# An encoder of two layers: the first q block goes ahead of the gate ranks, and the first expert group's weights come in four stages

## The reference, cut to what matters

```python
h = concat([meta, x])
for i in range(2):
    hn = rms_norm(h, norm_mix[i])
    h = h + (conv_gla_mixer(hn, sc_w_in, ...) if i == 0 else gqa_axial_mixer(hn, att_w_in, ...))
    h = h + hierarchical_moe(rms_norm(h, norm_ffn[i]), ...)
return rms_norm(h, norm_final)

# conv_gla_mixer: one product, then split into parts
a_b, a_c, a_x, q, k, v, r, g_f, g_b = split(hn @ w_in)      # g_f, g_b: gate ranks, 16 columns each
log_a_f = log_sigmoid(g_f @ wg_f + bg_f) / 16               # and log_a_b likewise

# hierarchical_moe: top group of 4, top 2 of its 8 experts
for e in range(32):
    he = silu(xt @ w_gate[e]) * (xt @ w_up[e])              # 1024 -> 256
    out += gates[:, e:e+1] * (he @ w_down[e])               # 256 -> 1024
```

## Time and profile before

| | |
|---|---|
| median of 3 runs | 718.74 us (717.98 to 719.11) |
| the profiled execution | 717.45 us |
| its span, first to last instruction | 715.6 us |
| busy: PE, VectorE, ScalarE, GpSimd | 627.2, 267.9, 183.3, 58.0 us |
| PE's share of the span | 88% |
| moved by DMA | 233.35 MB, 326 GB/s over the span |
| chain that ended last | PE 68%, DMA 15%, SP's queue 10%, VectorE 4% |

### The profile page before, as it was taken

The page is one execution under the profiler, slowest core; times in us unless marked ns, Lnnn a source line. Parts: engine busy times, 40 slices in busy tenths (PEclk is TensorE's granted clock), DMA queues, the critical chain, the costliest instruction groups (busy, mean ns, idle before and its releaser), DMA issues.

```text
span 715.6 us, 11273 instructions
## 1 busy us (share of the span) xinstructions
PE 627.2 (88%) x4780; PEld 404.1 (56%) x4780; DVE 267.9 (37%) x608; ACT 183.3 (26%) x371; POOL 58.0 (8%) x39
## 2 busy tenths in 40 slices
PE   5999999989899999699489999998899996677774
PEld 3698999967566474274134345677556463244331
DVE  6346348742222333033033488913313230211213
ACT  4554444342101010010005347823211010000003
POOL 1222222300000000000001450000000000000000
PEclk9999999998999999899799999999899998899888
DMA  9972337985899999999997615069999999999994
GB/s 312 277 254 111 118 119 259 419 308 244 355 420 399 423 421 421 420 422 420 411 387 270 240 54 177 1 226 424 397 398 419 419 422 419 423 420 420 422 402 169
DMA packets 58815, 233.35 MB, mean 326 GB/s; under 512 B 14402, under 2 KB 14708, under 8 KB 37252
## 3 DMA queue, kind: packets, MB, share of 16 engines
q1 hardware_dynamic: 56532, 232.32, 81.7%
q10 hardware_dynamic: 2224, 0.20, 0.2%
HBM read 231.44 MB, written 1.05 MB: 325 GB/s over the span
## 4 chain that ended last, share of the span: by engine, by line
PE 68%; DMA 15%; SPq 10%; DVE 4%; issue 2%; ACT 1%; ACTq 0%; DVEq 0%
PE bank L1975 11%; DMA ring<-in_moe_w_up 7%; PE bank L2040 6%; PE bank L2064 6%; PE bank L2013 5%; PE bank L1639 5%; SPq L415 5%; PE bank L1641 5%; PE bank L1640 5%; PE bank L2027 4%; PE bank L2129 4%; DMA ring<-in_moe_w_gate 4%; SPq L412 3%; PE bank L1660 2%; PE bank L2137 2%; DMA w_g<-in_sc_w_in 2%
## 5 line engine op out<-in xcount | busy, mean ns | idle before, releaser
L1975 PE MATMUL bank<-ring,hnT 128*32 128x256 f32 (+1 forms) x1480 | 128.3, 425 | 37.8 <-DMA ring<-in_moe_w_up 13.1
L1975 PEld LDWEIGHTS bank<-ring,hnT 128*32 128x32 f32 x1480 | 64.7, 118 | 81.2 <-issue 37.4
L2064 PE MATMUL bank<-moe_scratch 128*128 128x512 f32 (+1 forms) x160 | 79.0, 617 | 3.7 <-DVE moe_scratch L1406 2.0
L1374 DVE TENSOR_TENSOR h<-bank,h 128x512 f32<-128x512 f32 (+1 forms) x80 | 55.1, 689 | 55.0 <-PE bank L2064 54.8
L2013 PE MATMUL bank<-ring,moe_scratch 128*32 128x512 f32 x404 | 58.6, 596 | 1.0 <-ACT moe_scratch L858 0.5
L2040 PE MATMUL bank<-sel,hn 128*128 128x256 f32 x240 | 59.0, 405 | 0.0
L2040 PEld LDWEIGHTS bank<-sel,hn 128*128 128x128 f32 x240 | 57.9, 336 | 0.0
L1639 PE MATMUL bank<-hnT_hi,mix_hi 128*128 128x272 f32 x192 | 57.1, 298 | 0.0
L1391 DVE TENSOR_TENSOR moe_scratch<-moe_scratch,bank 128x256 f32<-128x256 f32 x16 | 6.7, 421 | 134.0 <-ACT moe_scratch L856 134.0
L1641 PE MATMUL bank<-hnT_lo,mix_hi 128*128 128x272 f32 x192 | 55.6, 289 | 0.0
L1640 PE MATMUL bank<-hnT_hi,mix_lo 128*128 128x272 f32 x192 | 55.3, 288 | 0.0
(11 more groups left out here) (327 smaller groups left out, 930.7 us busy)
## 6 DMA issues: line engine op xcount, KB each, us to landing
ring<-in_moe_w_gate SPq DMA_DIRECT2D x45, 1024.0 KB, 25.8
ring<-in_moe_w_down SPq DMA_DIRECT2D x44, 1024.0 KB, 17.8
ring<-in_moe_w_up SPq DMA_DIRECT2D x41, 1024.0 KB, 23.9
ring<-in_sc_w_in SPq DMA_DIRECT2D x12, 1024.0 KB, 11.5
tail<-in_moe_w_up SPq DMA_DIRECT2D x7, 1024.0 KB, 25.1
ring<-in_moe_w_gate SPq DMA_DIRECT2D x13, 512.0 KB, 7.2
ring<-in_moe_w_up SPq DMA_DIRECT2D x13, 512.0 KB, 8.3
ring<-in_moe_w_down SPq DMA_DIRECT2D x13, 512.0 KB, 18.1
```

Source lines behind the costliest of these rows:

```text
L1374: nc.vector.tensor_tensor(hh, B[[7, 4][k % 2]][0:n, :], hh, ALU.add).then_inc(sem(f"h_added{l}"), 1)
L1975: return mm(bank[at, :], xT[:, c, mine], right, start=(c == 0), stop=(c == KC - 1))
L2064: mm(B[[7, 4][k % 2]][0:m, :], selgT[:, TILE_AT[t]:TILE_AT[t] + m], y[:, half, :], start=True, stop=True).then_inc(sem(f"sc_ps{l}"), 1)
```

## The change

Three things change. The order at the start: the first q block (`q1st`) goes ahead of the gate ranks' product, the second q block is computed in one piece behind it, and the k block `raw_chunks(2)` takes its place between the gate tiles. The first group: a unit now holds two experts and a quarter of the features, two units make a stage, and there are four stages for gate and up, with the gather cut to match; a unit comes in four transfers of 256 KB with rows of 2 KB. The slot `ONCE` takes unit 7, of the fourth of these stages, so units 0 to 6 move one place up in the ring. The expert counts go behind the first quarter product. To have the semaphores for it, some that counted small transfers are merged: the gate parameters with the constants, the routing parameters with those of the attention, and two more pairs; and the weights of a layer use eight semaphores in turn, not six.

```diff
-            UNITS += [("gu", j, half) for half in range(2) for j in range(4)]
+            UNITS += [("gu", pair, part) for part in range(4) for pair in range(2)]
-    STAGES = [4, 4, 4] * NQ + [4]
+    STAGES = [2, 2, 2, 2, 4] + [4, 4, 4] * (NQ - 1) + [4]
-        return RING_ORDER[l][(i - 1) % RING[l]] if i else ONCE
+        return ONCE if i == LAST_GU else RING_ORDER[l][(i if i < LAST_GU else i - 1) % RING[l]]
...
-                    gu = dst.rearrange("p (u c n) -> p u c n", u=2, c=4)
-                    for u, name in enumerate(("moe_w_gate", "moe_w_up")):
-                        src = A[name][l, e].rearrange("(p c) n -> p c n", c=KC)[:, 4 * half:4 * half + 4, :]
-                        sp.dma_start(gu[:, u], src).then_inc(...)
+                    gu = dst.rearrange("p (e u c n) -> p e u c n", e=2, u=2, c=2)
+                    for k in range(2):
+                        for u, name in enumerate(("moe_w_gate", "moe_w_up")):
+                            src = A[name][l, 2 * e + k].rearrange("(p c) n -> p c n", c=KC)[:, 2 * half:2 * half + 2, :]
+                            sp.dma_start(gu[:, k, u], src).then_inc(...)
...
# first_units0: units 0, 1 | 12 to 17 | 2, 3 | 10, 11 | 4, 5 | 6, 7, 8, 9, 20   (before: 1, 2 | 12 to 17 | 3, 4 | 10, 11 | 5, 6 | 0, 7, 8, 9, 20)
# first_units1: units 20, 21 | 0 | 1 to 3 | 4, 5, 6, 8 to 12 | 13 to 16 | 7, 17, 18, 19   (before: 20, 21 | 1 | 2 to 4 | 5 to 12 | 13 to 16 | 0, 17, 18, 19)
...
             first_transposes()
-            pe.wait_ge(sem("w_g_in"), 16)
             pe.wait_ge(sem("hT_ready"), KC + 1)
-            for c in range(KC):
-                pe.wait_ge(sem("hn_ready"), c + 1)
-                last = mm(B[2][0:2 * RANK, 0:T], w_g[:, c, :], hn32[:, c, :], ...)
-            last.then_inc(sem("proj_ps"), 1)
...
             raw_chunks(0, B[3], range(0, KC))
-            pe.wait_ge(sem("q_ev"), 1)
-            pe.wait_ge(sem("gla_params_in"), 64)
+            pe.wait_ge(sem("w_g_in"), 16)
+            for c in range(KC):
+                last = mm(B[2][0:2 * RANK, 0:T], w_g[:, c, :], hn32[:, c, :], ...)
+            last.then_inc(sem("proj_ps"), 1)
+            raw_chunks(1, B[4], range(0, KC))
+            pe.wait_ge(sem("q_ev"), 2)
+            pe.wait_ge(sem("gla_in"), 80)
             gate_tile(0)
             for t in (1, 2):
-                raw_chunks(1, B[4], range(4 * t - 4, 4 * t))
+                raw_chunks(2, B[5], range(4 * t - 4, 4 * t))
                 gate_tile(t)
-            raw_chunks(2, B[5], range(0, KC))
             raw_chunks(3, B[6], range(0, KC))
...
-                def first_gate_up(r, half):
-                    wait_x(r, half + 1)
+                def first_gate_up(r, part):
+                    pe.wait_ge(sem(f"x_{('act', 'dve')[part % 2]}{l}"), r * NXE + part // 2 + 1)
...
                     first_gather(r, 0)
+                    first_gate_up(r, 0)
                     if first:
                         expert_loads()
-                    first_gate_up(r, 0)
-                    first_gather(r, 1)
+                    first_gather(r, 1, (0,))
                     first_gate_up(r, 1)
+                    first_gather(r, 1, (1,))
+                    first_gate_up(r, 2)
+                    first_gate_up(r, 3)
```

More of the change, by code:

```diff
@@ L68, in build_program @@
     ONCE = 19
+    LAST_GU = 7
     GAIN_AT = 15
-    NSEM = 6
+    NSEM = 8
     NSEL = NQ // 2 + 1
@@ L96, in landed @@
     def landed(stage):
-        same = [16 * STAGES[k] * (2 if k < 2 else 1) for k in range(stage % NSEM, NSTAGE, NSEM)]
+        same = [16 * STAGES[k] * (4 if k < 4 else 1) for k in range(stage % NSEM, NSTAGE, NSEM)]
         return sum(same[:stage // NSEM + 1]), sum(same)
@@ L304, in build_program @@
         PROJ, total = {}, 0
-        for kind, count in (("g", 1), ("q", 2), ("k", 2), ("v", 4), ("r", 4), ("ax", 4), ("ac", 4), ("ab", 4),
+        for kind, count in (("q1st", 1), ("g", 1), ("q", 1), ("k", 2), ("v", 4), ("r", 4), ("ax", 4), ("ac", 4), ("ab", 4),
                             ("out0", 8), ("kv", 3), ("q1", 2), ("q2", 2), ("out1", 4)):
@@ L422, in first_units0 @@
                 sp.wait_ge(sem("proj_ps"), PROJ["ac"] + 4)
-                for i in (1, 2):
+                for i in (0, 1):
                     unit(0, i)
@@ L428, in first_units0 @@
                 sp.wait_ge(sem("proj_ps"), PROJ["ab"] + 4)
-                for i in (3, 4):
+                for i in (2, 3):
                     unit(0, i)
@@ L435, in first_units0 @@
                 wait_mix_read(sp, 0, NMIX[0] - 2)
-                for i in (5, 6):
+                for i in (4, 5):
                     unit(0, i)
                 wait_mix_read(sp, 0, NMIX[0] - 1)
-                for i in (0, 7, 8, 9, 20):
+                for i in (6, 7, 8, 9, 20):
                     unit(0, i)
@@ L447, in first_units1 @@
                 sp.wait_ge(sem("kv_raw"), 3)
-                sp.dma_start(vm[32:32 + NM, 1, :], vm[0:NM, 0, :]).then_inc(sem("vm_in"), 16)
+                sp.dma_start(vm[32:32 + NM, 1, :], vm[0:NM, 0, :]).then_inc(sem("rest_in"), 16)
                 sp.wait_ge(sem("rstd_att"), 1)
-                unit(1, 1)
+                unit(1, 0)
                 wait_mix_read(sp, 1, 2)
-                for i in range(2, 5):
+                for i in range(1, 4):
                     unit(1, i)
                 sp.wait_ge(sem("oT_ps"), 8)
-                for i in range(5, 13):
+                for i in (4, 5, 6, 8, 9, 10, 11, 12):
                     unit(1, i)
@@ L461, in first_units1 @@
                 wait_mix_read(sp, 1, NMIX[1] - 1)
-                for i in (0, 17, 18, 19):
+                for i in (7, 17, 18, 19):
                     unit(1, i)
@@ L477, in later_params @@
                     for t in range(3):
[L478 to L481, removed]
@@ L1648, in _ @@
             first_transposes()
-            pe.wait_ge(sem("w_g_in"), 16)
             pe.wait_ge(sem("hT_ready"), KC + 1)
-            for c in range(KC):
-                pe.wait_ge(sem("hn_ready"), c + 1)
-                last = mm(B[2][0:2 * RANK, 0:T], w_g[:, c, :], hn32[:, c, :], start=(c == 0), stop=(c == KC - 1))
-            last.then_inc(sem("proj_ps"), 1)
             def raw_chunks(m, bank, chunks):
                 for c in chunks:
+                    pe.wait_ge(sem("hn_ready"), c + 1)
                     pe.wait_ge(sem(f"mix_w{c // 4}"), 16)
@@ L1725, in log_decays @@
                               (incl_fwd, incl_bwd)[dm // 2][0:n, 0:n], start=True, stop=True)
-                last.then_inc(sem("cum_ps"), 1)
+                last.then_inc(sem("gate_ps"), 1)
             for dm in range(3):
@@ L1975, in gate_up_product @@
                     return mm(bank[at, :], xT[:, c, mine], right, start=(c == 0), stop=(c == KC - 1))
-                def first_gate_up(r, half):
-                    wait_x(r, half + 1)
-                    w = [slots[at].rearrange("p (u c n) -> p u c n", u=2, c=4) for at in arrived(r, half)]
-                    for cc in range(4):
+                def first_gate_up(r, part):
+                    pe.wait_ge(sem(f"x_{('act', 'dve')[part % 2]}{l}"), r * NXE + part // 2 + 1)
+                    w = [slots[at].rearrange("p (e u c n) -> p e u c n", e=2, u=2, c=2) for at in arrived(r, part)]
+                    for cc in range(2):
                         for j in range(4):
-                            last = gate_up_product(0, 4 * half + cc, j, w[j][:, :, cc, :], B[2])
+                            last = gate_up_product(0, 2 * part + cc, j, w[j // 2][:, j % 2, :, cc, :], B[2])
                     last.then_inc(sem(f"stage_done{l}"), 1)
@@ L1990, in gate_up @@
                             wait_x(r, q + 2 if q == 1 else q + 3)
-                        w = [slots[at].rearrange("p (c n) -> p c n", c=KC) for at in arrived(r, 3 * q + u)]
+                        w = [slots[at].rearrange("p (c n) -> p c n", c=KC) for at in arrived(r, gate_up_stages(q)[u])]
                         for c in range(KC):
@@ L2021, in first_gather @@
                     width = SLOTS * (experts.stop - experts.start)
-                    for k in range(2):
+                    for k in parts:
                         for cc in range(2):
```

77 lines of the change are left out of this document (43 added, 34 removed).

## The result

The changed kernel takes 710.75 us (median of four executions, 710.20 to 711.64) beside 718.92 for the kernel before: 8.2 us faster, ratio 0.9895, 95% interval 0.9868 to 0.9922. The forecast was 4.4 us, 714.3.

A forecast was written before the change was run, and what follows sets the result against it. PE was taken to bound layer 0's mixer, the weight stream the end of each expert layer. Gains of 2.5 + 0.8 + 1.1 = 4.4 us off 718.74 gave 714.3 us, range 711.5 to 717.2.

The forecast's parts named there:

- Start: Layer 0's mixer start: q block first lets PE begin near 12.4 us instead of 14.82; gain 2.5 us.
- the cases that I had bounded: PE's pace in the first q block: slow until 17.98 us gains 1.8, slow throughout 1.0, fast throughout 4.8.
- costed at zero: At the start: gate tiles' wait for constants, later rank copy and gate logs, merged parameter semaphores; each 0 us.
- First group, layer 0: First expert group on PE: the 0.83 us wait before the second half product goes; gain 0.8 us, bounds 0.4 to 1.2.
- The stream dips longer near 220 us: Sign of a right forecast: layer 0's weight stream, dry again at 222 to 226 us, stays so longer.
- First group, layer 1: Layer 1's weight stream: two dips worth 1.44 us go, smaller transfers cost 0.3; gain 1.1, bounds 0.2 to 1.4.
- The case in which the forecast turns to a loss: Layer 1's stream: eight more transfers with unhidden fixed cost, from 0.6 us each; up to 731.6 us; chance 5%.
- The fixed 2.0 us: Per-transfer cost for layer 1's eight extra transfers, if paid in line: 16 us, giving 730.0 us.
- layer 0 ends 3.3 us earlier, and so does all that PE paces up to 470: Layer 0 from the 222 us dip on: the stream follows PE's 2.5 + 0.8 us lead, kept to 470 us.
- nothing is added to PE: At the start: two products of 16 records each merely swap places, with no added PE work.
- only the start counts: Finer groups gain nothing, as the stream dries out between stages and smaller transfers cost; 716.2 us, chance 15%.

The follow-up runs named there:

- before, again: The kernel before the change, run once more with no edit: 718.47 us.
- 4 idle: The kernel before plus four PE instructions that do nothing (waits on a semaphore long reached), ahead of layer 0's jump over further rounds: 716.90 us.
- 16 idle: The kernel before plus sixteen PE instructions that do nothing, ahead of the same jump in layer 0: 714.85 us, ratio 0.9954.
- start alone: The kernel before with only the new order at the start (first q block ahead of the ranks), groups as before; run twice: 712.72 and 713.32 us.
- groups alone: The kernel before with only the finer first expert group, start order as before, no idle instructions: 716.43 us, ratio 0.9994.
- groups alone, 16 idle: The changed kernel with its start order undone and sixteen PE instructions that do nothing ahead of the jump: 713.92 us, ratio 0.9951.
- after, twice: The full changed kernel, unedited, in two sets of executions: 710.75 us, then 711.82 us (ratios 0.9895 and 0.9925 to the kernel before).
- after, 223 idle: The changed kernel plus 223 PE instructions that do nothing, behind layer 0's first groups, ahead of the jump: 718.65 us, ratio 1.0005.
- after, 239 idle: The changed kernel plus 239 PE instructions that do nothing, behind layer 0's first groups, ahead of the jump: 711.91 us, ratio 0.9922.
- two transfers: The changed kernel with each first-group unit in two 512 KB transfers instead of four of 256 KB; run twice: 709.33 and 709.44 us.

## Why the prediction was wrong

With fourteen profiles at hand, each term can be measured between kernels that have a part and kernels that don't. All numbers are us from the traces.

| | start: log sums begin | first group, layer 0: gather to end | last group: product to scatter | layer 1's stream: first issue to last landing |
|---|---|---|---|---|
| before | 51.42 | 21.29 | 8.98, stall | 233.50 |
| before, again | 51.20 | 20.96 | 9.72, stall | 233.55 |
| 4 idle | 50.34 | 20.97 | 9.90, stall | 233.34 |
| 16 idle | 52.08 | 20.97 | 5.75 | 233.32 |
| start alone, twice | 49.16, 48.64 | 22.66, 20.97 | 4.99, 6.06 | 233.51, 233.59 |
| groups alone | 51.96 | 20.39 | 7.74, stall | 232.76 |
| groups alone, 16 idle | 51.21 | 20.39 | 5.94 | 232.87 |
| after, twice | 48.80, 47.08 | 20.38, 20.43 | 6.21, 5.77 | 233.48, 232.90 |
| after, 223 idle | 49.05 | 20.38 | 11.18, stall | 232.83 |
| after, 239 idle | 49.86 | 20.39 | 5.57 | 232.99 |
| two transfers, twice | 48.81, 49.87 | 20.66, 20.39 | 5.98, 6.22 | the end came from PE, 231.57 |

- **Start: right.** Forecast 2.5. The mean of the eight starts with the q block first is 48.91, of the six others 51.37: 2.5. The starts in the new order go from 47.08 to 49.87, so meeting it to a tenth is luck. The pace was the unknown, and it is what varies: q blocks of 3.90, 5.59 and 6.15 us stand for the cases that I had bounded. The gate tiles waited for nothing, and nothing else that I had costed at zero showed.
- **First group, layer 0: right in its mechanism, smaller.** Forecast 0.8, bounds 0.4 and 1.2; 20.97 against 20.39, the commonest of each, is 0.6. The stream dips longer near 220 us, as forecast (DMA share 0.56 and 0.65 in 216 to 224 after).
- **First group, layer 1: right in its mechanism, but half of its gain is gone at the end.** Forecast 1.44 for the dips less 0.3 for the transfers, 1.1. In the first 220 us of the stream, when dips and extra transfers are over, the six profiles with the old units have moved 90.27 to 90.35 MB, the six with four transfers a unit 90.70 to 90.92, the two with two transfers 91.02 and 91.03. On average that is 1.2 and 1.7 us ahead at 420 GB/s: the dips are worth 1.7, and eight more transfers cost 0.5, 0.06 each, between my bounds of 0 and 1.2. At the last landing less is left: the stream takes 233.47 on average with the old units, 232.97 with the new ones, 0.5. With two transfers a unit it took 231.57, in the one profile where it sets the end. The case in which the forecast turns to a loss, from 0.6 for each transfer, is far off. The fixed 2.0 us that the prediction takes for that case from the Trainium skill (DMA: Bandwidth & Descriptors, "Anatomy of one DMA") is given there for transfers that GpSimd issues. Here SP issues them.
- **The step that failed** is "layer 0 ends 3.3 us earlier, and so does all that PE paces up to 470". Up to the last group's gate product the step held, with 3.78; from the first scatter on the lead was 6.55, since the stall behind the jump went. With the stall, the product takes 9.50 us to the first scatter on average, without it 5.83: 3.7 us that stand in no term of the sum. I read the stretch up to 360 us only as a busy share in which the stream decides; the stall is one row of the waits, with the releaser "issue", and I didn't look at it. And "nothing is added to PE" was true of its records only: by count its program has 33 more instructions ahead of the jump, 31 of them in the start part, where each of the four raw products now waits for two semaphores a column (`hn_ready` and `mix_w`), not one. That they moved the jump's target out of the bad place is luck: nothing in the change was meant to do it.

The measured terms are 2.5 + 0.6 + 0.5 + 3.7 = 7.3, between the 5.4 and the 8.2 us of the two sets. Without the stall they are 3.6, less than the forecast of 4.4: its error would have been the other way. The rival "only the start counts" isn't refuted by times, since the group part alone can't be told from none; the traces give it 1.1.

What stays open: of the lead of 0.4 to 0.6 MB that the stream with four transfers has after 220 us in layer 1 (1.2 us on average) only 0.5 us is left at its end. The prediction let a lead early in the stream reach the end whole. Some of it is lost among the last eight down transfers: from SP's issue of the first to that of the last it takes 24.7 to 24.9 us with the old units, 25.3 to 25.8 in five of the six profiles with four transfers (24.65 in the other), 24.7 with two. Why wasn't tried. The start part alone falls 1 to 2 us short of what its two terms add up to (6.2), with no place in its profiles that shows it but the one slow stretch.

## What to carry to other kernels

Idle time with the releaser "issue", a few records behind a far jump in an engine's program, is worth a test of its own: a handful of idle instructions ahead of the jump shows whether the place decides, and can be worth more than the change in hand. A change that only moves work also shifts all code behind it, so measure each part with the jump's target held at a place without the stall, or a part gets credit that isn't its own, as the start part did here. Cut a transfer into finer stages by what each stage needs, but keep the number of transfers: two experts in one transfer kept the stages, and the stream's head as fast as it was.

## What the runs showed of the hardware

- PE stands still behind a jump for 2.17 to 4.43 us, with weights and buffers there; the place moves with PE's instructions (two to a record of these products: four idle ones moved it by two records) and comes back with 256 more. The executions with the stall move one 16 KB packet of instructions more (42 against 41, 43 against 42).
- It had time: before, PE waited 6.09 us for weights at the product's first record, and that wait didn't hide the stall. The packet of instructions that PE seems to have waited for came only after the product had begun.
- Eight more transfers, 256 KB instead of 512, cost 0.5 us of stream in all, 0.06 each, by the bytes moved in 220 us (90.82 MB on average against 91.02); halving the rows from 4 to 2 KB at 512 KB a transfer cost nothing that shows (325 to 327 and 328 GB/s over the first 14 us).
- The same start runs at different paces in different executions. The 6.15 us q block ran with a granted clock shown as 1.00 in 10 to 22 us, the 3.90 us one as well; for the 5.59 us one it is 0.72 in 10 to 16. So the slow pace of PE's first records isn't always to be seen in the granted clock.
